# Four attention layers, a mixer block and an expert layer on one core: scores in pairs, table load, latent turns, rotation and the experts' opening reordered

## The chip, the cores and the metric

One Trainium2 chip, one of its cores. The metric is the device time of one execution in microseconds, median of several. The profile of one execution stands beside it. Engines: TensorE (PE; its weight loads are PEld), VectorE (DVE), ScalarE (ACT), GpSimd (POOL) and SyncE (SP), which only issues DMAs here.

## The reference

256 tokens of width 1024, fp32. Four layers, each `x = layernorm(alpha * x + branch(x))`: MLA, windowed attention (SWA), forget-gated attention (FoX), MLA again. All have 16 heads and a silu gate ahead of the closing product.

```
MLA:   h = x @ w_in            -> latents cq (384), ckv (256), k_rope (32), gate (1024)
       q = rmsnorm(cq) @ w_q_up ; k, v = rmsnorm(ckv) @ w_kv_up ; the last 32 columns of
       q (per head) and k_rope are rotated ; causal softmax attention ; (o * silu(gate)) @ w_out
```

Then a second block: `h = modulate(x)` (rmsnorm, times gain and 1 + scale, plus shift, where scale and shift come from a conditioning product), a projection to pool input, q, k, v and gates, block attention over 8 heads (MoBA; with 256 tokens it is plain causal attention), a pool mixer, the merged product and `x = x + gate1 * (merged @ w_out)`. Last the experts (PEER): `h2 = modulate(x)`, `q = h2 @ w_q` (16 halves of 128), scores of each half against 128 keys, the top 16 of each, the top 16 of their sums, and then gelu of products with 16384 expert rows, gated and multiplied by the second table, and a final rmsnorm.

## The kernel before

All weights come as one stream of chunks (128 x 4 x 512), issued by SyncE in halves, the *pieces*. A piece is split into a high and a low part for exact fp32 products out of three fp32r products: ScalarE copies it to `w_hi` (L1210), VectorE subtracts to `w_lo` (L1526), TensorE multiplies (L698 to L700). There are four places for split pieces (RING); a piece is split as soon as TensorE has dropped the piece four earlier. What each engine does between splits is written out by hand: each engine has its own program, and the order in it is the order of the work. `evacuate(unit)` splits ahead until the unit's last piece, copies the unit out of its PSUM banks, and splits one further piece; `evacuate_only` copies alone; `split_ahead(n)` splits up to piece n + 4. `pieces_behind(closing, n)` is the nth piece behind a closing unit.

A `Unit` is one stretch of TensorE's work with one or two PSUM banks of a pair; units alternate between two pairs, and `bank_free` makes TensorE wait until the unit that had the pair before is copied. A unit of kind token has tokens on the partitions, of kind feature the output columns; a `turn` unit is transposes of token-major data by 128 columns. Where the turned data feeds a product, its copy is a split too: ScalarE writes `xT_hi` (L1259), VectorE subtracts to `xT_lo` (L1560).

**MLA** (layers 0 and 3). After the opening projection the latents, five tiles of 128 columns, are turned as a unit of four tiles and one of one tile, the rotated key part beside the latter. TensorE waits for the unit of four, projects three query units (two pieces each) and four key/value units (one piece each), turns the queries (four units of four heads), and starts the scores once keys, values and the first turned queries are copied. VectorE's program interleaves the copies of key/value units 0 and 1 with the rotations of the queries of block 0 and 1 (six operations each, L1683 to L1688).

**Attention.** One loop over heads, on each engine. On TensorE, turn i of the loop: scores of head i + 1, turn of the probabilities of head i - 1 (L895), outputs of head i - 2 (L903 to L905). VectorE scales and masks the scores and takes the row maximum (L1638), ScalarE takes the exponential (L1279) and copies the turned probabilities (L1292), VectorE divides the outputs by the row sum (L1652). `scores` (L854) does one head, `pair_scores` (L839) two, its products alternating between the two halves of 64 rows. SWA and FoX have a third score bank and use pairs from head 4 on; MLA (96 rows) and MoBA use `scores`. In MoBA, ahead of the loop on TensorE: first scores, value projection, pool mixer product; in turns 2 to 8 of the loop one k-step each of the merged product (`project_half`). On ScalarE a split up to the value unit's last piece stands ahead of the loop.

**Closing and the experts' opening.** The closing product is one unit of both blocks for columns 0 to 511, then block 0 and block 1 for the right half (`project_closing`, four shared pieces). VectorE adds each to x (`gate1`, L1599 and L1600), ScalarE squares a whole row of x of one block and takes the root (`mean_square`, L1307), VectorE inverts it and does four operations per block (`modulate_block`: x times root times scale, twice; plus shift, twice; L1743, L1745), then TensorE turns each half of the block (L787). The layers open with `project_opening`: block 0's products run before block 1 is turned. The experts' queries don't: all four turned halves are waited for, then four feature units follow, and the scores against the keys (L1107).

## Time and profile before

| | us |
|---|---|
| time, median of 3 | 1605.41 (1602.81 to 1608.67) |
| profiled execution, own time | 1602.43 |
| its span | 1600.6 |
| TensorE busy | 1529.7 |
| VectorE busy | 1095.5 |
| ScalarE busy | 811.1 |
| mean granted TensorE clock | 0.995 of full |

The span runs from the first to the last instruction. Layers 0 to 3 end at about 578 us, the mixer block at 752, the experts' queries at 809, their scores at 817; the selection of experts runs beside the first table's products until about 960. A matmul's busy time overlaps with the next one's, so starts are to be compared, not ends. A row of the timeline merges like instructions (x count); in brackets is the idle time of the engine before it and what ended it.

### The profile page before, as it was taken

Reading aid. Unit: us, or ns where it says so; the run is one execution under the profiler, and the core shown is the slowest. Engines: PE = TensorE matmul, PEld = TensorE weight load, DVE = VectorE, ACT = ScalarE, POOL = GpSimd, SP = SyncE. Lnnn points to the kernel's source line nnn. Section 1 sums busy time; section 2 is a strip of 40 time slices with the busy share of each in tenths; the row PEclk is TensorE's granted clock in tenths of the full one; section 3 lists DMA queues with packets and bytes.
Section 4 is the critical chain, followed back from the end, with each engine's and each line's share of the span. In section 5 each row is a group of like instructions: output and inputs, shape, how many; then the busy total and the mean of one; then the engine's idle time right before and its main releaser. Section 6 shows DMA issues by size and latency. Waiting matters only on the chain.

```text
span 1600.6 us, 30066 instructions
## 1 busy us (share of the span) xinstructions
PE 1529.7 (96%) x10694; PEld 1331.6 (83%) x10694; DVE 1095.5 (68%) x2204; ACT 811.1 (51%) x1352; POOL 79.7 (5%) x110
## 2 busy tenths in 40 slices
PE   6989999999998989998999999999999999999997
PEld 5867877896787768776999999999998888888886
DVE  3566656656667485458569997777778888865555
ACT  3665465446547544454356666334444444444554
POOL 1000600100010100000000000000000000000000
PEclk9999999999999999999999999999999999999999
DMA  6553654656356556424535556444444445465552
GB/s 244 180 170 118 224 184 140 218 187 235 132 183 212 197 176 237 152 91 160 197 132 174 180 171 204 150 157 160 163 161 158 164 164 170 164 244 195 195 190 101
DMA packets 78501, 281.44 MB, mean 176 GB/s; under 512 B 9408, under 2 KB 11488, under 8 KB 77152
## 3 DMA queue, kind: packets, MB, share of 16 engines
q1 hardware_dynamic: 74176, 261.97, 48.4%
q0 software_dynamic: 4256, 18.56, 3.4%
q8 instruction: 41, 0.67, 0.2%
q14 instruction: 28, 0.23, 0.0%
HBM read 277.31 MB, written 2.14 MB: 175 GB/s over the span
## 4 chain that ended last, share of the span: by engine, by line
PE 76%; DVE 16%; ACT 3%; issue 3%; DMA 2%; POOL 0%; ACTq 0%; DVEq 0%; POOLq 0%
PE banks L698 21%; PE banks L700 21%; PE banks L699 21%; DVE w_lo L1526 5%; PE banks L1131 3%; PE banks L895 2%; PE banks L854 2%; PE banks L815 1%; PE banks L793 1%; PE banks L905 1%; DMA arena<-x_spill 1%; PE banks L904 1%; DVE arena L2010 1%; ACT w_hi L1210 1%; PE banks L903 1%
## 5 line engine op out<-in xcount | busy, mean ns | idle before, releaser
L1210 ACT ACTIVATE w_hi<-raw 128x1024 fp32r<-128x1024 f32 x456 | 474.0, 1042 | 549.0 <-PE banks L700 518.8
L1526 DVE TENSOR_TENSOR w_lo<-raw,w_hi 128x1024 fp32r<-128x1024 f32 x456 | 547.5, 1205 | 268.6 <-ACT w_hi L1210 265.3
L698 PE MATMUL banks<-w_hi,xT_hi 128*128 128x512 f32 (+2 forms) x1140 | 444.1, 390 | 15.5 <-DVE w_lo L1526 11.4
L700 PE MATMUL banks<-w_hi,xT_lo 128*128 128x512 f32 (+2 forms) x1140 | 437.1, 383 | 0.0
L699 PE MATMUL banks<-w_lo,xT_hi 128*128 128x512 f32 (+2 forms) x1140 | 436.7, 383 | 0.0
L698 PE MATMUL banks<-xT_hi,w_hi 128*128 128x256 f32 x1392 | 397.7, 286 | 4.6 <-DVE w_lo L1526 1.7
L699 PE MATMUL banks<-xT_lo,w_hi 128*128 128x256 f32 x1392 | 394.2, 283 | 0.0
L700 PE MATMUL banks<-xT_hi,w_lo 128*128 128x256 f32 x1392 | 394.1, 283 | 0.0
L698 PEld LDWEIGHTS banks<-xT_hi,w_hi 128*128 128x128 f32 x1392 | 267.4, 192 | 6.5 <-issue 4.1
L699 PEld LDWEIGHTS banks<-xT_lo,w_hi 128*128 128x128 f32 x1392 | 267.6, 192 | 0.2
L700 PEld LDWEIGHTS banks<-xT_hi,w_lo 128*128 128x128 f32 x1392 | 267.3, 192 | 0.0
L698 PEld LDWEIGHTS banks<-w_hi,xT_hi 128*128 128x128 f32 x1140 | 215.3, 189 | 61.7 <-DVE w_lo L1526 8.9
L700 PEld LDWEIGHTS banks<-w_hi,xT_lo 128*128 128x128 f32 x1140 | 215.2, 189 | 42.9
L699 PEld LDWEIGHTS banks<-w_lo,xT_hi 128*128 128x128 f32 x1140 | 215.6, 189 | 40.0 <-issue 0.2
L2081 DVE TENSOR_TENSOR arena<-arena,banks 128x512 f32 (+1 forms) x64 | 44.1, 689 | 76.6 <-PE banks L1131 73.8
L2073 DVE TENSOR_TENSOR scratch<-scratch 128x512 bf16<-128x512 bf16 x192 | 69.8, 419 | 0.0
L1259 ACT ACTIVATE arena<-banks 128x512 f32<-128x512 f32 (+3 forms) x74 | 41.0, 578 | 56.1 <-PE banks L700 38.8
L1279 ACT ACTIVATE scratch<-scratch,neg_max 128x128 f32<-128x128 f32 (+1 forms) x144 | 63.6, 444 | 2.2 <-DVE neg_max L1638 2.1
L1131 PEld LDWEIGHTS banks<-scratch 128*128 128x128 bf16 x1536 | 50.0, 98 | 9.7 <-issue 8.3
L1292 ACT ACTIVATE scratch<-banks 128x384 f32<-128x384 f32 x72 | 35.1, 488 | 44.8 <-PE banks L895 44.5
L1131 PE MATMUL banks<-scratch 128*128 128x64 bf16 x1536 | 57.7, 193 | 0.0
L895 PEld LDWEIGHTS banks<-kept,scratch 128*128 128x128 f32 x216 | 22.5, 140 | 39.8 <-issue 21.2
(195 smaller groups left out, 1284.6 us busy)
## 6 DMA issues: line engine op xcount, KB each, us to landing
raw<-stream SPq DMA_DIRECT2D x490, 512.0 KB, 3.6
arena<-ln_in POOLq DMA_DIRECT2D x4, 1024.0 KB, 5.8
arena<-x_spill POOLq DMA_DIRECT2D x3, 1024.0 KB, 10.7
arena<-mod_rows POOLq DMA_DIRECT2D x2, 1536.0 KB, 8.1
raw<-stream SPq DMA_DIRECT2D x6, 256.0 KB, 4.0
arena<-g_in POOLq DMA_DIRECT2D x3, 512.0 KB, 11.8
raw<-stream SPq DMA_DIRECT2D x8, 160.0 KB, 2.4
arena<-arena POOLq DMA_DIRECT2D x2, 512.0 KB, 4.3
```

The costliest lines, as they stand in the source:

```text
L698: pe.matmul(out, stationary[0], moving[0], start=first, stop=False, **k)
L699: pe.matmul(out, stationary[0], moving[1], start=False, stop=False, **k)
L700: return pe.matmul(out, stationary[1], moving[0], start=False, stop=last, **k)
L895: mm = pe.transpose(banks[:, 6 + g % 2, c * P:(c + 1) * P], probs[:, g % 2, c * P:(c + 1) * P], ident)
L1131: mm = pe.matmul(banks[:, 4 + s // GATE_STEPS, t * HALF:(t + 1) * HALF], hot2[:, t // 2, :, t % 2], hot1[:, part, t // 2, :, t % 2], start ...
L1210: act.activation(part(w_hi[:, s]), part(half_raw(s), True), ACT.Copy).then_inc(piece_hi, 1)
L1259: act.activation(dst, src, fn).then_inc(evac_act, 1)
L1279: ins = act.activation(probs[:, g % 2, lo:hi], s_sb[:, g % 2, lo:hi], ACT.Exp, scale=-1.0, bias=neg_max[:, g % 4, b:b + 1], accum_out=row_ ...
L1292: act.activation(probsT[:, g % 2], banks[:, 6 + g % 2, 0:384], ACT.Copy).then_inc(probsT_ready, 1)
L1526: dve.tensor_tensor(part(w_lo[:, s]), part(half_raw(s), True), part(w_hi[:, s].bitcast(F32)), ALU.subtract).then_inc(piece_lo, 1)
L2073: ins = dve.tensor_tensor(hot1[:, part], match1, picks[2 + part].broadcast_to(mine), ALU.mult)
L2081: dve.tensor_tensor(mine, mine, banks[:, 4 + s // GATE_STEPS, 0:GT * HALF].rearrange("p (t n) -> p n t", t=GT), ALU.mult).then_inc(g_taken ...
```

## The change

Six edits, all of them in the order of work, none in what is computed.

1. Latents: turned in units of two, two and one tiles; the first query unit gets a wait between its two pieces.
2. MLA, VectorE: each rotation stands ahead of the copy of key/value unit 0 or 1; the split behind the last key/value copy is left to a later place.
3. A dummy exponential (`exponential_table`) on ScalarE: in MLA between the second and third turned query unit, in MoBA ahead of the loop.
4. Scores: SWA and FoX do heads 2 and 3 as a pair in turn 0; MoBA does all heads in pairs, with two banks, and a pair waits for both masks of the pair before. MoBA's split ahead of ScalarE's loop moves behind the second exponential.
5. The experts' opening: the squares go by halves, the left ones once the left columns are there; x times scale is taken before the root, one half of it on GpSimd, and one fused operation per half remains behind the root; splits of pieces are placed anew; the first query unit becomes a token unit opened by blocks.
6. That unit's queries are turned (four tiles) after the second query unit; scores wait accordingly.

```diff
@@ -268,7 +268,7 @@
-peer = dict(h=cut(6144, B, D), qT=cut(8192, 2 * PEER_HEADS, S), keys=cut(12288, 2 * PEER_HEADS * NKEYS),
+peer = dict(h=cut(6144, B, D), q=cut(18432, B, COLS), qT=cut(8192, 2 * PEER_HEADS, S), keys=cut(12288, 2 * PEER_HEADS * NKEYS),
@@ -291,6 +291,7 @@
+squares = cut(8192, B, D)
@@ -314,8 +315,8 @@
-def feature_units(dst, tiles, how=COPY2):
-    return [Unit(plan, "feature", [dst[:, t:t + 2], dst[:, t + 2:t + 4]], how, pieces=4) for t in range(0, tiles, 4)]
+def feature_units(dst, tiles, how=COPY2, t0=0):
+    return [Unit(plan, "feature", [dst[:, t:t + 2], dst[:, t + 2:t + 4]], how, pieces=4) for t in range(t0, t0 + tiles, 4)]
@@ -351,9 +352,11 @@
-        L["cT"] = split_turn_units(5)
-        L["krT"] = [Unit(plan, "turn", [mla["krT"][0:ROPE, 0:1]], [("act", "copy")], tiles=1, width=ROPE, pair=L["cT"][1].pair,
-                         at=1, after=(L["cT"][1].before,))]
+        first = Unit(plan, "turn", [(0, 2)], [("both", "split")], tiles=2)
+        other = Unit(plan, "turn", [(2, 4)], [("both", "split")], col0=2, tiles=2, pair=first.pair, at=1, after=(first.before,))
+        L["cT"] = [first, other, Unit(plan, "turn", [(4, 5)], [("both", "split")], col0=4, tiles=1)]
+        L["krT"] = [Unit(plan, "turn", [mla["krT"][0:ROPE, 0:1]], [("act", "copy")], tiles=1, width=ROPE, pair=L["cT"][2].pair,
+                         at=1, after=(L["cT"][2].before,))]
@@ -421,7 +424,10 @@
-E["q"] = feature_units(peer["qT"], 2 * PEER_HEADS)
+E["q"] = token_units(peer["q"], COLS)
+E["q"] += feature_units(peer["qT"], 4, t0=4)
+E["qT"] = turn_units(peer["qT"], 4)
+E["q"] += E["qT"] + feature_units(peer["qT"], 8, t0=8)
@@ -459,6 +465,7 @@
+scale_ready, h_scaled = sem("scale_ready"), sem("h_scaled")
@@ -666,6 +673,9 @@
+    pool.wait_ge(scale_ready, 1)
+    wait_put(pool, M["out"][2:3])
+    pool.tensor_tensor(peer["h"][:, 1, COLS:D], x_tok[:, 1, COLS:D], moba["mod"][:, 4, COLS:D], ALU.mult).then_inc(h_scaled, 1)
@@ -830,10 +840,10 @@
-        if h == 4:
+        if third is not None and h == 4:
...
-            pe.wait_ge(max_ready, g - 1 if h else g)
+            pe.wait_ge(max_ready, g - 1 if third is not None and h > 2 else g)
@@ -882,7 +892,7 @@
-    def attention(heads, q, k, v, ada=(), late=(), beside=(), gated=None, third=None):
+    def attention(heads, q, k, v, ada=(), late=(), beside=(), gated=None, third=None, paired=False):
@@ -911,9 +921,9 @@
-            if third is not None and i >= 3:
-                if i % 2 and i + 1 < heads:
-                    pair_scores(i + 1, q, k, third)
+            if paired:
+                if i in (0, *range(3, heads - 1, 2)):
+                    pair_scores(max(i + 1, 2), q, k, third)
@@ -969,7 +979,8 @@
-            for u in L["q_up"]:
+            project(L["q_up"][0], between=lambda: wait_put(pe, L["cT"][1:2]))
+            for u in L["q_up"][1:]:
@@ -1010,7 +1021,7 @@
-                      third=third_bank(L))
+                      third=third_bank(L), paired=True)
@@ -1031,7 +1042,7 @@
-                      ada=(4, 6, 8, 10, 12, 14), late=L["late"], gated=(l, attn["o"]), third=third_bank(L))
+                      ada=(4, 6, 8, 10, 12, 14), late=L["late"], gated=(l, attn["o"]), third=third_bank(L), paired=True)
@@ -1064,7 +1075,7 @@
-    first_scores(queries, keys)
+    first_scores(queries, keys, paired=True)
@@ -1074,7 +1085,8 @@
-    attention(MOBA_HEADS, queries, keys, lambda h, b: moba["v"][:, b, HD * h:HD * (h + 1)], late=M["mixT"], beside=M["pool"])
+    attention(MOBA_HEADS, queries, keys, lambda h, b: moba["v"][:, b, HD * h:HD * (h + 1)], late=M["mixT"], beside=M["pool"],
+              paired=True)
@@ -1092,11 +1104,12 @@
-    for n, u in enumerate(E["hT"]):
-        pe.wait_ge(h_half, 4 + n + 1)
-        turn(u, peer["h"])
-    wait_put(pe, E["hT"])
-    for u in E["q"]:
+    open_layer(E["q"][0], E["hT"], h_half, 4, peer["h"])
+    project(E["q"][1])
+    wait_put(pe, E["q"][0:1])
+    for u in E["qT"]:
+        turn(u, peer["q"])
+    for u in E["q"][3:]:
@@ -1260,7 +1273,7 @@
-    def attention(heads, kind, last=None, mix=None, beside=()):
+    def attention(heads, kind, last=None, mix=None, beside=(), behind=None):
@@ -1279,6 +1292,8 @@
+            if i == 1 and behind is not None:
+                behind()
@@ -1308,9 +1323,24 @@
+    def square_half(b, half):
...
+        c = slice(half * COLS, (half + 1) * COLS)
+        link(act.activation(squares[:, b, c], x_tok[:, b, c], ACT.Square, accum_out=small[:, 48 + 2 * b + half:49 + 2 * b + half]))
+        if half == 0:
+            link(act.activation(small[:, 52 + b:53 + b], small[:, 48 + 2 * b:49 + 2 * b], ACT.Identity, bias=small[:, 5:6],
+                                scale=1.0 / D))
+        else:
+            act.activation(small[:, 40 + b:41 + b], small[:, 49 + 2 * b:50 + 2 * b], ACT.Sqrt, bias=small[:, 52 + b:53 + b],
+                           scale=1.0 / D).then_inc(dev_ready, 1)
...
...
+    def exponential_table():
...
+        act.activation(small[:, 45:46], small[:, 4:5], ACT.Exp)
@@ -1350,7 +1380,10 @@
-            for u in L["kv_up"] + L["qT"]:
+            for u in L["kv_up"] + L["qT"][:2]:
+                evacuate(u)
+            exponential_table()
+            for u in L["qT"][2:]:
@@ -1395,8 +1428,9 @@
-    split_ahead(M["v"][0].pieces_done - 1)
-    attention(MOBA_HEADS, "moba", last=M["v"][0], mix=M["mixT"][0], beside=M["pool"])
+    exponential_table()
+    attention(MOBA_HEADS, "moba", last=M["v"][0], mix=M["mixT"][0], beside=M["pool"],
+              behind=lambda: split_ahead(M["v"][0].pieces_done - 1))
@@ -1406,14 +1440,18 @@
+    wait_put(act, M["out"][0:1])
+    for b in range(B):
+        square_half(b, 0)
+    pieces_behind(M["out"], 1)
...
-    mean_square(0)
-    for n in range(1, RING):
+    square_half(0, 1)
+    for n in range(2, RING):
...
-    mean_square(1)
+    square_half(1, 1)
@@ -1831,15 +1869,16 @@
-                evacuate(L["kv_up"][b])
...
-            for u in L["kv_up"][B:]:
-                evacuate(u)
+                evacuate(L["kv_up"][b])
+            evacuate(L["kv_up"][2])
+            split_ahead(L["kv_up"][3].pieces_done - 1)
+            evacuate_only(L["kv_up"][3])
@@ -1929,25 +1968,47 @@
+    dve.wait_ge(g2_loaded, 32)
+    dve.wait_ge(mod_loaded, 32)
+    gain_scale(moba["mod"][:, 4])
+    dve.sem_inc(scale_ready, 1)
...
-    dve.wait_ge(g2_loaded, 32)
-    dve.wait_ge(mod_loaded, 32)
-    gain_scale(moba["mod"][:, 4])
+    wait_put(dve, out[0:1])
...
+    left, right = slice(0, COLS), slice(COLS, D)
...
+    def scaled(b, c):
+        note(dve.tensor_tensor(peer["h"][:, b, c], x_tok[:, b, c], moba["mod"][:, 4, c], ALU.mult))
...
+    def rooted(b):
...
+        settle()
+        inverse_root(small[:, 40 + b:41 + b], small[:, 42 + b:43 + b])
+        if b:
+            dve.wait_ge(h_scaled, 1)
+        for c in (left, right):
+            dve.scalar_tensor_tensor(out=peer["h"][:, b, c], in0=peer["h"][:, b, c], scalar=small[:, 42 + b:43 + b],
+                                     in1=moba["mod"][:, 3, c], op0=ALU.mult, op1=ALU.add).then_inc(h_half, 1)
...
+    for b in range(B):
+        scaled(b, left)
...
-    wait_put(dve, out[0:2])
-    modulate_block(peer["h"], moba["mod"][:, 4], moba["mod"][:, 3], 0)
+    wait_put(dve, out[1:2])
+    scaled(0, right)
+    rooted(0)
+    pieces_behind(out, 1)
...
-    modulate_block(peer["h"], moba["mod"][:, 4], moba["mod"][:, 3], 1)
-    pieces_behind(out, 1)
+    pieces_behind(out, 3)
+    rooted(1)
+    pieces_behind(out, RING)
...
-    pieces_behind(out, RING)
```

## Rows read from the trace of the kernel before

**Rows 1.** The page: busy time (share) xinstructions by engine; then two instruction groups.

```profile
PE 1529.7 (96%) x10694; PEld 1331.6 (83%) x10694; DVE 1095.5 (68%) x2204; ACT 811.1 (51%) x1352; POOL 79.7 (5%) x110
...
L1210 ACT ACTIVATE w_hi<-raw 128x1024 fp32r<-128x1024 f32 x456 | 474.0, 1042 | 549.0 <-PE banks L700 518.8
...
L1526 DVE TENSOR_TENSOR w_lo<-raw,w_hi 128x1024 fp32r<-128x1024 f32 x456 | 547.5, 1205 | 268.6 <-ACT w_hi L1210 265.3
```

**Rows 2.** Windows of 20 us: length, busy time of each engine, PEclk, DMA.

```profile
840.00:860.00 20.00, 20.00 (x169) 20.00 (x168) 19.83 (x64) 14.23 (x18) 0.00 (x0) 1.00 0.51 170
```

**Rows 3.** Timeline, first MLA layer, latents: start, us, instruction [idle <-releaser].

```profile
60.91 1.62 DVE L1560 TENSOR_TENSOR xT_lo<-banks,xT_hi 128x512 fp32r<-128x512 f32 x3 [0.93 <-ACT xT_hi L1259]
...
62.45 0.48 PE L698 MATMUL banks<-w_hi,xT_hi 128*128 128x512 f32 x1 [1.70 <-DVE xT_lo L1560]
```

**Rows 4.** Timeline, first MLA layer, keys, values and turned queries.

```profile
81.22 0.42 DVE L1683 TENSOR_TENSOR arena<-arena 128x256 f32<-128x256 f32 x1
...
83.48 0.69 DVE L1575 COPY arena<-banks 128x512 f32<-128x512 f32 x1
...
84.28 0.36 PE L698 MATMUL banks<-xT_hi,w_hi 128*128 128x256 f32 x1 [0.65 <-issue]
...
88.43 1.05 PE L793 MATMUL banks<-kept,arena 128*96 128x128 f32 x8 [1.05 <-DVE arena L1575]
...
91.84 1.55 PE L854 MATMUL banks<-arena 96*128 96x128 f32 x8 [0.63 <-ACT arena L1259]
```

**Rows 5.** Timeline, first MLA layer, start of attention.

```profile
95.79 1.28 ACT L1279 ACT_TABLE_LOAD   x1
...
98.12 0.55 PE L895 MATMUL banks<-kept,scratch 128*128 128x128 f32 x3 [0.85 <-ACT scratch L1279]
```

**Rows 6.** Timeline, scores of window attention, and of block attention.

```profile
219.20 0.92 PE L854 MATMUL banks<-arena 64*128 64x128 f32 x4
...
221.42 0.47 ACT L1292 ACTIVATE scratch<-banks 128x384 f32<-128x384 f32 x1
...
222.75 0.93 PE L839 MATMUL banks<-arena 64*128 64x128 f32 x8
...
670.71 0.93 PE L854 MATMUL banks<-arena 64*128 64x128 f32 x8
```

**Rows 7.** Timeline of block attention, then one window (PE busy, PEclk, DMA).

```profile
687.36 0.89 PE L854 MATMUL banks<-arena 64*128 64x128 f32 x4 [1.12 <-issue]
...
699.03 0.92 PE L854 MATMUL banks<-arena 64*128 64x128 f32 x4
...
689.00:692.50 3.50, 3.50 (x12) 0.51 0.45 150
```

**Rows 8.** Timeline of the experts' opening, then one window.

```profile
748.11 1.06 ACT L1307 ACTIVATE arena<-arena 128x1024 f32<-128x1024 f32 x1 [4.75 <-DVE arena L1600]
...
752.42 0.69 DVE L1599 TENSOR_TENSOR scratch<-banks,arena 128x512 f32<-128x512 f32 x1
...
755.58 1.41 DVE L1743 SCALAR_TENSOR_TENSOR arena<-arena,small 128x512 f32<-128x512 f32 x2
...
757.65 1.97 PE L787 MATMUL banks<-kept,arena 128*128 128x128 f32 x8 [4.43 <-DVE arena L1745]
...
761.15 0.55 PE L698 MATMUL banks<-xT_hi,w_hi 128*128 128x256 f32 x1 [1.53 <-DVE xT_lo L1560]
...
760.50:764.00 3.50, 2.85 (x13) 0.50 0.61 208
```

**Rows 9.** Timeline: GpSimd's 512-column product; experts' query copies; first score product.

```profile
388.87 1.27 POOL L602 TENSOR_TENSOR arena<-arena 128x512 f32<-128x512 f32 x1 [36.41 <-DVE arena L1652]
...
797.27 0.69 DVE L1575 COPY arena<-banks 128x512 f32<-128x512 f32 x1 [0.56 <-PE banks L700]
...
808.79 0.69 DVE L1575 COPY arena<-banks 128x512 f32<-128x512 f32 x1 [0.56 <-PE banks L700]
...
809.64 0.57 PE L1107 MATMUL banks<-arena 128*128 128x128 f32 x3 [0.89 <-DVE arena L1575]
```

## The prediction

> **What bounds the kernel now.** I read the page first: TensorE is busy 1529.7 of 1600.6 us, so all that a reordering can win lies in the 71 us in which it is not, plus products that can be run side by side [rows 1]. Then the stretches of 20 us: from 820 us on TensorE is full, and VectorE sits at 19.8 of 20 us in the selection of experts (840 to 860) [rows 2]. Last the timeline, gap by gap, with what released TensorE. The reader is to see in each row the idle time in brackets: it is what an edit can remove at that place, and no more. Since every stage up to 820 us hands its end directly to the next one on TensorE, a gap closed there moves all that follows; the selection starts from the expert scores, so it moves too and takes nothing back.
>
> **Latents by two tiles** (two MLA layers). Eight transposes take 1.05 us [rows 4], so four take 0.5. Before, the first copy waits for all eight; now it waits for four. TensorE sat 1.70 us before the first query product, until VectorE had subtracted the second pair of tiles, begun at 60.91 [rows 3]. With ScalarE still copying the last gate columns, the chain starts about 0.45 us sooner. The wait put between the two query pieces buys nothing more: the first query unit lies in the bank pair of the second latent unit, and its own wait for free banks covers that unit already. 0.45 us per layer (0 to 1.0).
>
> **Rotation ahead of copies.** A rotation is six operations of 0.42 us, 2.2 us with their links [rows 4]. Now both stand ahead of the copies of keys and values: VectorE at about 77.8 rotates to 80.1, copies unit 0 (0.69) to 80.8, splits a piece (1.2 us [rows 1]) to 82.0, rotates to 84.3, copies unit 1 to 85.0. The bank of unit 1 is what the last unit waits for: it started at 84.28 after 0.65 idle [rows 4] and now starts at about 85.1, ending at 88.0 instead of 87.3. What is queued behind this wait is only that unit and the turns. But the copy of unit 2 is then over (86.9), the rotation too, and the turn of queries starts at 88.05 instead of 88.43. The second turn waits for ScalarE's key copy of the last unit until 89.4 instead of 90.16. The split that stood between the last value copy and the first query copy on VectorE is deferred, so the first scores, at 91.84 before, wait only for ScalarE's copy of the first queries, at about 91.1. Gain 0.75 per layer (bounds: loss of 0.8, if the late last unit is paid in full, to gain of 1.7, the idle of 1.05 and 0.63 together). The deferred split frees the landing place of the second piece-pair of conditioning weights, needed only at head 5, some 8 us later: no cost, about 1 us if that cover were gone.
>
> **Exponential's table ahead** (both MLA layers). The load takes 1.28 us at 95.79 and ScalarE's first exponential follows it at once; TensorE is idle 0.85 before it turns the first probabilities [rows 5]. The load now falls where ScalarE waits for turned queries (91.6 to 93.1). After it TensorE's own order is dense: 0.85 per layer (0 to 1.28). Together the MLA layers give 2 x (0.45 + 0.75 + 0.85) = 4.1 us. A rule speaks here: the Trainium skill (ScalarE: Activation LUTs, "What ACT_TABLE_LOAD costs") gives 1283 ns and about 1380 ns of drain for a switch. The trace agrees on the load and shows no drain: the exponential began by 97.1, as its result left TensorE free at 98.12. By the rule the load removed would be 2.66 us, but the idle time behind it, 0.85, still caps the sum. In the block attention the moved load was under the value projection anyway: nothing.
>
> **Paired scores.** One head's scores are 0.92 us of TensorE, two heads issued as a pair 0.93 [rows 6]: 0.9 us per pair if TensorE is the bound there. In the window and forget layers only heads 2 and 3 are newly paired. There TensorE's next need is ScalarE's copy of head 0's turned probabilities, 221.42 to 221.89 [rows 6], and ScalarE works without a break from its table load on; so 0 (0 to 0.9 each). In the block attention heads 0 and 1 already took 0.93 together, one behind the other in different halves of the array [rows 6]: 0. For heads 2 and 3 the wait that ends last is the one for the mixed pool tiles, which frees TensorE at 687.36 [rows 7]. It stays, but head 3's 0.9 us now lie ahead of it, in place of idle time: 0.9. Heads 4 to 7 are in the stretch where scores, turn, outputs and half projection follow one another without a gap (687.36 and 699.03 are such heads) [rows 7]: 2 x 0.85. The new wait (both masks of the pair before) has behind it the turn, the outputs and the half projection of its turn of the loop; the mask of head 3 needs only the exponential of head 1, which now is done before the value projection ends. Sum 2.6 (0.9 to 3.5). TensorE's clock was granted at 0.51, the 1.2 GHz level, from 689 to 692.5 [rows 7]; I leave that as it is, since the idle ahead of it stays about 1.4 us. If it went, 3.5 us at half the clock would give back 1.7 more.
>
> **The experts' opening.** Before: the second residual unit is ready at 752.42; two pairs of gating operations, a square of 1.06 us, root, two scalings and two shifts end in the third turn at 757.65, after 4.43 us idle; the products begin at 761.15, after 1.53 idle and at a clock of 0.50 until 764 [rows 8]. After, step by step. Block 0: ScalarE now takes a piece (1.04 us) before the right half's square, so that the root comes at about 750.1 and the half-ready signals at 751.1 and 751.9: in time for 752. VectorE then splits a piece (1.2) that it did not before, and starts the second residual at 753.1, 0.7 late; it ends at 754.5, the two subtractions for block 0 at 755.2 and 755.9. TensorE can now start block 0's products at 755.35: idle 2.2. Two more splits stand ahead of block 1's scaling (to 758.4), reciprocal and two fused operations (0.7 each, from 1.41 for two [rows 8]) give signals at 759.45 and 760.1. TensorE has three pieces' worth of block 0 to do (4.3 us plus 0.5 waiting for the second piece), so it arrives at about 760.0 and waits for nothing. Then the last piece's split (to 761.35) holds it 0.4, and the subtractions for block 1 end at 762.8. A unit is 808.79 - 797.27 = 11.52 us [rows 9], so block 1's half is 5.76 and the first unit ends at 768.5. Before, it ended one unit and the slow part later: three more units led to 808.79, so it ended at 774.2. That is 5.7 gained, less eight more transposes (1.05, clear of waits because the banks are the first unit's, copied long before), plus the 0.89 before the first score product, which now needs the unit before the last: 5.5 us. The added right-half product on GpSimd is like the one of 1.27 us [rows 9]: 754.6 to 755.9, wanted at 758.4; behind it on that queue stands only the spill of x, which is wanted after the scores, 50 us later. Were that cover gone, 1.3. The gain scaling (1.2) moves to where VectorE waits for pieces: 0. Bounds: 2.0, if block 1's splits and signals come 3 us late, to 7.0, if the 2.2 idle shrinks by VectorE's early split being free.
> A rule speaks against the GpSimd part: the Trainium skill (GPSIMD Engine Reference, "1. Specifications") says that GpSimd shares its SBUF interfaces with VectorE, with contention where VectorE reads two SBUF inputs. The subtractions that run then read one input from PSUM, and no row shows the collision; by the rule at its worst the 1.3 us would be added to VectorE's order and the whole sum be 10.9 instead of 12.2.
>
> **Sum.** 4.1 + 2.6 + 5.5 = 12.2 us. The profiled execution took 1602.4 us (span 1600.6 and 1.8 around it), so it would be 1590.2; the median of three was 1605.4, 3.0 above the profiled one. Against the median: 1593.2 us.
>
> **Rivals.**
> A. The low clock stays at the experts' opening. For it: idle of 4.43 brought it [rows 8]. Against: idle of 1.70 did not [rows 3], and 2.2 lies nearer to that. Price: the low level held from the third turn (1.97 us instead of 1.05 for eight transposes) until 764, some 7 us at half the clock [rows 8], so 3.5 us. Time 1596.7.
> B. The new order bites in the MLA layers (late last unit in full, -0.8, no gain before the scores) and the opening is bound by VectorE (2.0): 2 x (0.45 - 0.8 + 0.85) + 2.6 + 2.0 = 5.6. Time 1599.8. For it: VectorE gets three splits ahead of block 1's signals.
> C. The change does not do what it says where overlap was there before: the pairs give nothing (as for heads 0 and 1), MLA half, opening 2.0: 4.0, no more than the measurement can tell. Time 1601.4.
> D. Slower: TensorE stays at the low level through the experts' queries, because block opening breaks its activity up. Four units of 11.5 us at half the clock would add 46 us; it decides from 24.4 us at the low level on, where it eats the 12.2 us. Time with 35 us of it, 17.5 lost: 1610.7. Against: before, the clock came back 3 us after the products had begun, and they ran on without a break [rows 8].
>
> **Numbers.** Forecast 0.57, A 0.18, B 0.12, C 0.10, D 0.03. The forecast's own range, from the bounds, is 1590 to 1597. Holding the time 8 in 10, with a noise of the median of some 2.5 us: 1587.5 to 1600.0. About 0.3%, 4.8 us, is what a measurement can tell from no change; faster is the forecast, A and B but for a little: 0.86; same: 0.11; slower: D, 0.03.
>
> **What would show it.** The gap before the query products in MLA about 1.2 instead of 1.7; the first MLA scores 0.75 us plus that 0.45 earlier than 91.84; table loads ahead of the turned queries and no gap of 0.85; four pairs of 0.93 in block attention; third turn of the experts' opening without 4.4 us idle, no 0.50 clock there, first unit done about 16.5 us after the last residual product. The prediction is wrong if the idle time merely moves to the next wait, above all if TensorE waits for split pieces in the opening.

## The result

The changed kernel takes 1589.01 us (median of 4 runs, 1586.35 to 1591.61), the kernel before 1604.74 (median of 4). The ratio is 0.9897, with a 95% interval of 0.9883 to 0.9912: 16.5 us less by the ratio, 15.7 by the two medians. The forecast was 1593.2, the range 1587.5 to 1600; the narrower range that the prediction calls its own was 1590 to 1597, and the time lies 1 us below it. A later set of four runs gave a median of 1589.56 and a ratio of 0.991 (0.9893 to 0.9926); the median of all eight is 1589.56 too. The first profiled execution took 1586.35 us, its span 1584.0, against 1602.43 and 1600.6 before; it is the fastest of the eight, so what is read from its profile is what this one execution did.

The busy line of the changed kernel's page, to be laid beside [rows 1]: TensorE is busy 8 us less (two products of a pair run side by side, and less work falls into a stretch at the low clock); the rest of the 16.6 is idle time. The window that answers to [rows 2] is as full as it was.

```profile
PE 1521.7 (96%) x10653; PEld 1325.5 (84%) x10654; DVE 1094.8 (69%) x2204; ACT 812.7 (51%) x1362; POOL 80.9 (5%) x111
```

```profile
823.00:843.00 20.00, 20.00 (x169) 20.00 (x168) 19.83 (x66) 13.87 (x17) 0.00 (x0) 1.00 0.51 164
```

Timeline of the changed kernel, first MLA layer (start, duration, instruction, and in brackets the idle time with what released it), to be laid beside [rows 3 to 5]. The reader is to see the 1.70 us become 0.97, the 0.65 before the last kv unit become 1.00, the turn of queries without its 1.05, the table load ahead at 91.00, and the first probabilities without their 0.85.

```profile
62.16 0.47 PE L708 MATMUL banks<-w_hi,xT_hi 128*128 128x512 f32 x1 [0.97 <-DVE xT_lo L1598]
...
84.58 0.36 PE L708 MATMUL banks<-xT_hi,w_hi 128*128 128x256 f32 x1 [1.00 <-issue]
...
87.53 1.03 PE L803 MATMUL banks<-kept,arena 128*96 128x128 f32 x8
...
90.55 1.58 PE L864 MATMUL banks<-arena 96*128 96x128 f32 x8 [0.48 <-ACT arena L1272]
...
91.00 1.28 ACT L1343 ACT_TABLE_LOAD   x1
...
95.84 0.49 PE L905 MATMUL banks<-kept,scratch 128*128 128x128 f32 x3
```

Window and forget attention ([rows 6]): the pair of eight products is there, and two new idles stand behind it.

```profile
216.97 0.93 PE L849 MATMUL banks<-arena 64*128 64x128 f32 x8
...
218.87 0.55 PE L905 MATMUL banks<-kept,scratch 128*128 128x128 f32 x3 [0.49 <-ACT scratch L1292]
...
219.72 0.43 PE L913 MATMUL banks<-arena,scratch 128*128 128x64 f32 x2 [0.30 <-ACT scratch L1307]
```

Block attention ([rows 6, 7]): four pairs, one idle of 1.39, and the clock at 1.00 where it had been 0.51.

```profile
678.61 0.93 PE L849 MATMUL banks<-arena 64*128 64x128 f32 x8
...
681.40 0.52 PE L905 MATMUL banks<-kept,scratch 128*128 128x128 f32 x3 [1.39 <-issue]
...
683.91 0.93 PE L849 MATMUL banks<-arena 64*128 64x128 f32 x8
...
689.70 0.93 PE L849 MATMUL banks<-arena 64*128 64x128 f32 x8
...
682.00:689.00 7.00, 7.00 (x47) 5.70 (x47) 3.89 (x23) 4.86 (x16) 0.00 (x0) 1.00 0.24 77
```

The experts' opening ([rows 8, 9]). VectorE's early split (741.48) holds the last residual copy until 742.62, 0.5 late (0.7 foreseen; 752.42 before, less the 10.34 gained up to here); the products start after 2.66 us idle and run on without another wait, at full clock; the first score product has no 0.89 ahead of it.

```profile
741.48 1.22 DVE L1564 TENSOR_TENSOR w_lo<-raw,w_hi 128x1024 fp32r<-128x1024 f32 x1
...
742.62 0.68 DVE L1637 TENSOR_TENSOR scratch<-banks,arena 128x512 f32<-128x512 f32 x1
...
744.18 1.26 POOL L678 TENSOR_TENSOR arena<-arena 128x512 f32<-128x512 f32 x1 [19.88 <-DVE arena L1638]
...
744.24 1.29 DVE L1598 TENSOR_TENSOR xT_lo<-banks,xT_hi 128x512 fp32r<-128x512 f32 x2 [0.21 <-DVE arena L1638]
...
745.19 0.47 PE L708 MATMUL banks<-w_hi,xT_hi 128*128 128x512 f32 x1 [2.66 <-DVE xT_lo L1598]
...
750.51 0.50 PE L708 MATMUL banks<-w_hi,xT_hi 128*128 128x512 f32 x1
...
745.00:755.00 10.00, 9.81 (x46) 7.87 (x47) 7.05 (x10) 3.28 (x6) 1.00 (x2) 1.00 0.75 277
...
793.07 7.20 PE L1120 MATMUL banks<-arena 128*128 128x128 f32 x63
```

The two traces as a ledger. A stage's gain is how much the difference of starts, before minus after, grows across it; the two last columns put back one part of the change at a time (below), from the same places of its profile and from its median, against 1589.56. A median is the weaker measure here: the 95% interval of the opening's ratio below, 0.9912 to 0.9956, is 7 us wide.

| stage | predicted | two profiles | put back, profile | put back, median |
|---|---|---|---|---|
| start, to 59 us | 0 | -0.15 | | |
| MLA, first | 2.05 | 2.43 | 2.37 | both: 5.9 |
| window attention | 0 | -0.08 | 0.0 | both: -0.4 |
| forget attention | 0 | 1.03 | 0.15 | |
| MLA, second | 2.05 | 2.59 | 2.55 | |
| block attention | 2.6 | 4.5 | 6.1 | 4.6 |
| experts' opening | 5.5 | 6.2 | 6.4 | 4.1 |
| after it | 0 | 0.1 | | |
| sum | 12.2 | 16.6 | | |

The sum is the span's difference, 1600.6 less 1584.0. To be explained are 0.9 us that were not expected of MLA, 1.0 that forget attention should not have had, 1.9 in block attention and 0.7 at the opening.

### The profile page after: what moved, and what is told of

It is laid out like the page before. It is cut to its first block, busy times and chain, and to the rows that moved or that the text cites. A ratio compares the mean times of both kernels' runs of the same rounds, so it can differ in the third digit from the quotient of the medians.

```text
span 1584.0 us, 30009 instructions
## 1 busy us (share of the span) xinstructions
PE 1521.7 (96%) x10653; PEld 1325.5 (84%) x10654; DVE 1094.8 (69%) x2204; ACT 812.7 (51%) x1362; POOL 80.9 (5%) x111
## 4 chain that ended last, share of the span: by engine, by line
PE 80%; DVE 14%; ACT 2%; issue 2%; DMA 0%; POOL 0%; ACTq 0%; DVEq 0%; POOLq 0%
PE banks L708 23%; PE banks L710 22%; PE banks L709 22%; DVE w_lo L1564 5%; PE banks L1144 3%; PE banks L905 2%; PE banks L864 1%; PE banks L825 1%; PE banks L803 1%; PE banks L915 1%; PE banks L914 1%; PE banks L849 1%; DVE arena L2071 1%; PE banks L913 1%; ACT w_hi L1223 1%
## 5 line engine op out<-in xcount | busy, mean ns | idle before, releaser
L708 PE MATMUL banks<-w_hi,xT_hi 128*128 128x512 f32 (+2 forms) x1156 | 450.1, 389 | 16.8 <-DVE w_lo L1564 10.8
L710 PE MATMUL banks<-w_hi,xT_lo 128*128 128x512 f32 (+2 forms) x1156 | 443.2, 383 | 0.0
L709 PE MATMUL banks<-w_lo,xT_hi 128*128 128x512 f32 (+2 forms) x1156 | 442.5, 383 | 0.0
L708 PE MATMUL banks<-xT_hi,w_hi 128*128 128x256 f32 x1360 | 388.1, 285 | 3.9 <-issue 2.0
L709 PE MATMUL banks<-xT_lo,w_hi 128*128 128x256 f32 x1360 | 384.6, 283 | 0.0
L710 PE MATMUL banks<-xT_hi,w_lo 128*128 128x256 f32 x1360 | 384.5, 283 | 0.0
L708 PEld LDWEIGHTS banks<-xT_hi,w_hi 128*128 128x128 f32 x1360 | 260.6, 192 | 5.9 <-issue 5.2
L709 PEld LDWEIGHTS banks<-xT_lo,w_hi 128*128 128x128 f32 x1360 | 260.8, 192 | 0.2
L710 PEld LDWEIGHTS banks<-xT_hi,w_lo 128*128 128x128 f32 x1360 | 260.6, 192 | 0.0
L1690 DVE TENSOR_TENSOR arena<-banks,row_sum 128x128 f32<-128x128 f32 x72 | 21.0, 292 | 48.9 <-PE banks L915 48.1
```

Source lines behind the costliest of these rows:

```text
L708: pe.matmul(out, stationary[0], moving[0], start=first, stop=False, **k)
L709: pe.matmul(out, stationary[0], moving[1], start=False, stop=False, **k)
L710: return pe.matmul(out, stationary[1], moving[0], start=False, stop=last, **k)
```

## The experiments

Each kernel is the changed one with the edit shown; the profiled execution of each is read by the same stages. "Late" is how much later than in the first profile of the changed kernel something starts. Where only one run is given, the stages of its profile count and not its time.

**The opening put back.** Both edits of the opening are undone: token queries by whole units, ScalarE's and VectorE's old order, eight transposes fewer.

```diff
-            open_layer(E["q"][0], E["hT"], h_half, 4, peer["h"])
+            for n, u in enumerate(E["hT"]):
+                pe.wait_ge(h_half, 4 + n + 1)
+                turn(u, peer["h"])
+            wait_put(pe, E["hT"])
...
-            rooted(0)
-            pieces_behind(out, 1)
+            modulate_block(peer["h"], moba["mod"][:, 4], moba["mod"][:, 3], 0)
```

> Both edits of the experts' opening are undone (the queries' unit again by whole tokens, the pieces' splits and the eight transposes back in their old order); the layers keep the new order. If the opening is worth what the two traces show between the end of the MoBA projection and the first score product of the experts, this runs 6.2 us over the changed kernel (5.5 by the prediction). The stretch at the low clock ahead of the experts' queries should be back if it hangs on VectorE's whole-token unit: then 6 to 7 us, with a wait of over 4 us on the products' operand. If the low clock stays away without the edit, 4 to 5 us and the rest of the gain belongs to the clock. Nothing of it should be given back later: the last product should end by the same difference.

Measured: 1593.64 us (median of 5, ratio to before 0.9934, 0.9912 to 0.9956), 4.1 over the changed kernel. Its profile is 1.05 late at the end of the MoBA projection and 7.44 at the first score product: 6.4. The timeline and a window of that stretch:

```profile
748.35 1.82 PE L791 MATMUL banks<-kept,arena 128*128 128x128 f32 x8 [4.43 <-DVE arena L1772]
...
751.70 0.55 PE L702 MATMUL banks<-xT_hi,w_hi 128*128 128x256 f32 x1 [1.53 <-DVE xT_lo L1587]
...
749.00:754.50 5.50, 3.97 (x19) 3.60 (x18) 5.32 (x6) 1.19 (x2) 0.00 (x0) 0.50 0.36 119
```

The idle of 4.43, the slow turn and the low clock are back exactly as in [rows 8]. Nothing is given back later (7.5 at 944 us).

**Whole-token queries in the new order.** Here only the block opening is undone; pieces and roots keep their new order.

```diff
-            open_layer(E["q"][0], E["hT"], h_half, 4, peer["h"])
+            for n, u in enumerate(E["hT"]):
+                pe.wait_ge(h_half, 4 + n + 1)
+                turn(u, peer["h"])
+            wait_put(pe, E["hT"])
+            project(E["q"][0])
```

> The experts' queries' unit keeps the new order of the work ahead of it but opens by whole tokens, not by blocks. If the blocks give most of the gain (the prediction: products start 5.8 us earlier), products start some 3 to 5 us later than in the changed kernel, and the first score product of the experts 3 to 4 us later. If the low clock ahead of the experts' queries hangs on the length of that wait, it comes back and adds 1 to 2 us. Rival: the shorter chain of the root gives most: 1 to 2 us and no low clock.

Measured: 1595.47 us in one run. The products start 7.1 us later than in the changed kernel (753.19 less the 0.93 by which this profile was late before the stage, against 745.19), the first score product 8.2, and the wait at 953.00 (943.81 in the changed kernel) 8.3. That is twice what was expected, 3 to 5 and 3 to 4.

```profile
749.69 1.97 PE L797 MATMUL banks<-kept,arena 128*128 128x128 f32 x8 [6.18 <-DVE arena L1996]
...
753.19 0.76 PE L708 MATMUL banks<-w_hi,xT_hi 128*128 128x512 f32 x1 [1.53 <-ACT xT_hi L1276]
...
749.00:758.00 9.00, 6.78 (x19) 5.37 (x20) 3.82 (x5) 1.20 (x2) 0.00 (x0) 0.50 0.62 218
```

That is worse than the old opening (6.4): the two splits ahead of block 1 make a whole-token turn later, 6.18 idle instead of 4.43, and pay only where block 0's products cover them. The low level also lasts longer, about 10 us for 6.8. The blocks are the gain; what is left of the two edits without them is a loss of 1.8 (8.2 against 6.4), and the rival falls. The squares by halves and the early scaling were not put back by themselves.

**GpSimd's product back on VectorE.**

```diff
-            pool.wait_ge(scale_ready, 1)
-            wait_put(pool, M["out"][2:3])
-            pool.tensor_tensor(peer["h"][:, 1, COLS:D], ...).then_inc(h_scaled, 1)
...
+            scaled(1, right)
```

> Only the product of the right half of the second token tile goes back from GpSimd to VectorE, 0.7 us of VectorE's time. If VectorE's order sets the start of the experts' queries, they start 0.7 us later and so does the first score product of the experts. Rival: VectorE waits at that place for something else (the reciprocal's root or the last product), and it costs 0 to 0.2. A shared way into the memory for the two engines, had it been paid in the changed kernel (its product took 1.26 us beside two of VectorE's subtractions), would make VectorE's part shorter here: under 0.5 us.

Measured: 1591.04 us in one run, and from 3.28 to 3.91 late across the opening, 0.63. But not where it was expected: the queries start with the same idle, and the product of 0.68 pushes the split behind it, for which TensorE waits 0.52 in front of the second piece.

```profile
747.52 1.29 DVE L1595 TENSOR_TENSOR xT_lo<-banks,xT_hi 128x512 fp32r<-128x512 f32 x2 [0.21 <-DVE arena L1635]
...
748.72 0.68 DVE L1980 TENSOR_TENSOR arena<-arena 128x512 f32<-128x512 f32 x1
...
748.47 0.47 PE L705 MATMUL banks<-w_hi,xT_hi 128*128 128x512 f32 x1 [2.65 <-DVE xT_lo L1595]
...
750.59 0.50 PE L705 MATMUL banks<-w_hi,xT_hi 128*128 128x512 f32 x1 [0.52 <-DVE w_lo L1561]
```

VectorE's two subtractions take 1.29 us here, without GpSimd's product, and 1.29 beside it in the changed kernel (744.24, above), so running beside each other cost nothing. The Trainium skill (GPSIMD Engine Reference, "1. Specifications") tells of contention where VectorE reads two SBUF inputs; each of these subtractions reads one of its inputs from PSUM (`banks`), so that case is not tested here.

**Block attention put back,** then its two parts. First all of it:

```diff
-            first_scores(queries, keys, paired=True)
+            first_scores(queries, keys)
...
-            exponential_table()
-            attention(MOBA_HEADS, ..., behind=lambda: split_ahead(M["v"][0].pieces_done - 1))
+            split_ahead(M["v"][0].pieces_done - 1)
+            attention(MOBA_HEADS, ...)
```

> MoBA alone is undone: each head's scores singly again, the exponential's table and the piece split in their old order; MLA, SWA, FoX and the opening of the experts keep the new order. Theory: the 4.5 us that this layer gained in the traces are 2.6 us of edits and some 1.5 to 1.9 us of a low-clock stretch that the edits remove, so it runs 4.5 us over the changed kernel and the low clock at about 683 us is back. Rival: the low clock was a matter of where the stretch fell in the execution, and it stays away: 2.6 to 3 us over. Second rival: ScalarE's copies are the need in all of it, as in SWA: 0 to 1 us.

Then the pairs alone (the first part of that edit and `paired=True` of the attention loop), and ScalarE's order alone (the second part):

> In MoBA only the pairing of the scores is undone; ScalarE's work keeps the new order (the table ahead, the piece split behind). The prediction gives the pairs all of the MoBA gain: 0.9 for heads 2 and 3, 0.85 each for two of the later pairs, 2.6 us, and the low clock at about 683 us with them. The layer's edits undone together cost 6.1 us in the traces, low clock included. Theory: the pairs are 2.6 us plus the clock, so 4 to 6 us from the first scores to the end of the projection, with the low clock back. Rival: the order on ScalarE carries a part: under 2 us and no low clock.

> In MoBA only ScalarE's order is undone (the split of the weights' piece ahead of the heads again, the table not ahead); the pairs stay. Theory: the order of ScalarE lies under TensorE's turns, 0 to 0.5 us from the first scores to the end of the projection, and no low clock. Rival: the 1.9 us that MoBA gained over the 2.6 of the prediction are ScalarE's: 1 to 2 us later, with idle ahead of the first turn of probabilities and the low clock at about 683 us back.

Measured: all of it 1594.13 us (median of 5, ratio 0.9939, 0.9914 to 0.9965), 4.6 over, and 6.1 in its profile; the pairs alone 6.0 (one run, 1595.06); ScalarE's order 0.2 (one run, 1589.48). All of the layer's gain is the pairs'. The low clock is back with single scores, and earlier than before; with the pairs kept and ScalarE in its old order (third block) it is not:

```profile
682.13 1.52 PE L864 MATMUL banks<-arena 64*128 64x128 f32 x4 [1.12 <-issue]
...
683.00:688.50 5.50, 5.50 (x18) 3.89 (x17) 1.77 (x11) 2.23 (x9) 0.00 (x0) 0.50 0.29 98
```

```profile
683.07 1.50 PE L864 MATMUL banks<-arena 64*128 64x128 f32 x4 [1.40 <-issue]
...
683.00:690.00 7.00, 6.93 (x22) 5.27 (x23) 2.71 (x11) 2.51 (x10) 0.00 (x0) 0.51 0.25 77
```

```profile
683.07 0.52 PE L905 MATMUL banks<-kept,scratch 128*128 128x128 f32 x3 [1.12 <-issue]
```

Three profiles now have single scores, with the low level for about 3.4, 6.8 and 6.8 us (summed over windows of 2 us), and the layer costs 4.5, 6.1 and 6.0 us more than with pairs. So nearly 0.5 us is lost per us at the low level ((6.1 - 4.5) / (6.8 - 3.4)), and what is left without it is about 2.9 us, where the prediction had 2.6. Rows at the full clock give the same 2.9: two single heads take 2 x 3.39 us (in the kernel before, 695.64 below to 699.03 in [rows 7]), two paired ones 5.79 (683.91 to 689.70 above), so a pair is worth 0.99, not 0.85, twice, and heads 2 and 3 give the 0.9.

```profile
695.64 0.92 PE L854 MATMUL banks<-arena 64*128 64x128 f32 x4
```

In none of the eleven profiles with pairs was the clock low between 676 and 720 us. What keeps it up isn't the idle time ahead. The cleanest comparison is ScalarE's old order with pairs and without: both have 1.12 us of idle and the same busy time of TensorE in the 6 us ahead of the next product (4.53 and 4.56), and only without pairs is the clock low behind it. In the changed kernel it is 1.39 idle and 4.61 busy, with the pairs alone undone 1.40 and 4.67. The windows of the changed kernel, of all put back, and of ScalarE's order put back:

```profile
675.40:681.40 6.00, 4.61 (x26) 3.31 (x25) 3.64 (x7) 3.29 (x7) 0.00 (x0) 1.00 0.57 197
```

```profile
676.10:682.10 6.00, 4.56 (x22) 3.19 (x21) 3.49 (x7) 5.99 (x16) 0.00 (x0) 1.00 0.43 152
```

```profile
677.07:683.07 6.00, 4.53 (x26) 3.19 (x25) 3.48 (x7) 5.99 (x16) 0.00 (x0) 1.00 0.45 156
```

One thing in them does go with the edit: the number of products, 26 with pairs, 22 or 23 without, since a pair puts eight score products where one head has four. No run shows whether that is the cause.

**MLA put back,** all three edits, then two of them singly.

```diff
-                    for u in L["kv_up"] + L["qT"][:2]:
-                        evacuate(u)
-                    exponential_table()
-                    for u in L["qT"][2:]:
+                    for u in L["kv_up"] + L["qT"]:
                         evacuate(u)
...
                     for b in range(B):
+                        evacuate(L["kv_up"][b])
...
-                        evacuate(L["kv_up"][b])
-                    evacuate(L["kv_up"][2])
-                    split_ahead(L["kv_up"][3].pieces_done - 1)
-                    evacuate_only(L["kv_up"][3])
+                    for u in L["kv_up"][B:]:
+                        evacuate(u)
```

> The MLA edits are undone (latents by one tile, rotation behind the copies, the exponential's table behind the queries' units), in both MLA layers. The prediction had 4.1 us for the two; the traces show 2.45 and 2.55 from the layer's start to its end, so this runs 4.9 us over the changed kernel. Rival: part of what the first layer shows is the clock at the start of the execution, which differs between the two profiles: then the sum is 4 us or less, and the idle of 1.70 us ahead of the queries' opening is not all back.

> Only the exponential's table in the two MLA layers is undone (loaded again behind all four queries' units). By the prediction's step the first turn of probabilities waits again, idle of 0.85 us ahead of it in each layer, so it starts 0.85 us later against the layer's first scores; from the layer's start to its end 0.85 each, 1.7 in both. Rival: with the rotation ahead the queries' units end earlier on ScalarE too, so part of the load is hidden: 0 to 0.5 each. A drain of 1.4 us in front of the load, had ScalarE one, would put it at 1.28 plus 1.38 behind the last copy: over 1.5 us of idle instead of 0.85.

> Only the order of VectorE's work behind the rotation in MLA is undone (the rotation of the kv tiles and queries again behind the copies). The prediction had 0.75 us per layer of this edit: the wait ahead of the last kv unit goes from 1.00 back to 0.65 us, 0.45 ahead of the queries' turns comes back (1.05 us of idle), and the first scores start later. The traces say 1.29 less 0.29, about 1.0 us at the first scores. So 0.75 to 1.0 per layer later at the first scores. Rival: the gain is carried by the table, and with it ahead the first probabilities start no later: 0 at the layer's end.

Measured: all three 1595.44 us (median of 6, ratio 0.994, 0.9921 to 0.9959), 5.9 over; its profile has 2.37 and 2.55 in the two layers, and 1.2 of a low clock at the experts' opening that is not the edit's. The table alone (1591.16 us, one run) costs 1.00 and 1.16; the rotation alone (1589.74, one run) 0.97 at the first probabilities of the first layer (in the second, a low clock at 506 to 511 us lies over it). The rest, 0.45, is the latents by two tiles, which were not put back by themselves: from the latents' turn to the query opening the profile of all three put back goes from 0.61 to 1.06 late, and those of the two single edits stay as late as they were. First the table's rows, then the rotation's:

```profile
95.04 1.28 ACT L1292 ACT_TABLE_LOAD   x1
...
97.37 0.55 PE L905 MATMUL banks<-kept,scratch 128*128 128x128 f32 x3 [0.76 <-ACT scratch L1292]
```

```profile
83.48 0.36 PE L708 MATMUL banks<-xT_hi,w_hi 128*128 128x256 f32 x1 [0.65 <-issue]
...
87.63 1.05 PE L803 MATMUL banks<-kept,arena 128*96 128x128 f32 x8 [1.04 <-DVE arena L1613]
```

The load starts when the activation before it ends, and takes 1.28; TensorE waits 0.76, but 1.00 is lost: with the table ahead the probabilities' turn starts 0.76 behind the start of the scores before it (95.08 to 95.84), here 1.67 (95.70 to 97.37). The products' own 0.92 overlaps with what follows when nothing waits, and the idle in brackets does not count that 0.15. A drain beside the load, of which the Trainium skill speaks (ScalarE: Activation LUTs, "What ACT_TABLE_LOAD costs"), is in no row: the activation ahead of the load ends at 95.02, the load starts at 95.04, and the exponential behind it at 96.34.

**The pair of heads 2 and 3** in window and forget attention put back.

```diff
-                    if paired:
+                    if third is not None and i in (0, 2):
+                        scores(i // 2 + 2, q, k)
+                    elif paired:
```

> Only the pair of heads 2 and 3 in SWA and FoX is undone; all else is the changed kernel. Theory: ScalarE's copy of head 0's probabilities is the need of the product behind, so the pair gives nothing (0 in both layers), and the 1.03 us that FoX gained in the traces are the raw pieces of the weights that landed late in the profile before: the same time as the changed kernel within 0.3 us. Rival: the pair gives FoX its 1.0 us and more would come in SWA without its waits: 1.0 us over the changed kernel, with idle of 0.28 and 0.30 us ahead of the two probability turns gone.

Measured: 1589.11 us (median of 4, ratio 0.9899, 0.9869 to 0.9929), no difference; across window attention 0.0, across forget attention 0.15, with the two idles gone. The singly issued score at 219.34 fills the wait that the pair leaves:

```profile
219.34 0.92 PE L864 MATMUL banks<-arena 64*128 64x128 f32 x4
...
220.76 0.43 PE L913 MATMUL banks<-arena,scratch 128*128 128x64 f32 x2
```

**The changed kernel again, and three more moves.** The repeat shows what belongs to an execution.

> The changed kernel again, beside the next one on the same chip: 15 to 16.5 us under the kernel before. It serves as the mark for the next kernel, and its profile shows which of the differences between the two first profiles belong to the execution: the low clock at 24 to 28 us, and the 1.03 us in FoX. If FoX's 1.03 is of the edits, its stage takes as long as in the first profile of the changed kernel (98.70 us from 283.25 to 381.95); if it is the landing of the weights' pieces, it takes anything from 98.7 to 99.8.

Forget attention took 98.70 us in the first profile of the changed kernel and 99.47 in the repeat; others with the same code of this layer took between 98.7 and 99.7 where the clock stayed up, the kernel before 99.78. What differs is ScalarE's wait for weights that the stream has not landed. The same piece in the kernel before, in the repeat, and in the first profile, where it had landed and TensorE's banks were the wait:

```profile
372.72 1.06 ACT L1210 ACTIVATE w_hi<-raw 128x1024 fp32r<-128x1024 f32 x1 [2.60 <-DMA raw<-stream]
```

```profile
370.03 1.06 ACT L1223 ACTIVATE w_hi<-raw 128x1024 fp32r<-128x1024 f32 x1 [2.24 <-DMA raw<-stream]
```

```profile
369.58 1.06 ACT L1223 ACTIVATE w_hi<-raw 128x1024 fp32r<-128x1024 f32 x1 [1.66 <-PE banks L710]
```

So some 0.9 of the 1.1 us by which the stage differs is landing (2.60 less 1.66), not the change. The repeat also had a low clock at the experts' opening that the first profile had not; it lost 1.3 us there (0.66 late at the turn ahead of it, 1.98 at the first score product):

```profile
747.00:750.00 3.00, 3.00 (x9) 2.19 (x8) 2.96 (x6) 0.00 (x0) 0.00 (x0) 0.52 0.99 350
```

Another stretch cost nothing. At the opening of the block attention layer TensorE waits 4.5 us in every profile, and in all fourteen the clock is low behind it, for some 3.4 us in eight and 6.8 in six. The first profile of the changed kernel, then the repeat:

```profile
574.00:577.00 3.00, 3.00 (x10) 2.13 (x9) 2.96 (x6) 1.20 (x2) 0.00 (x0) 0.50 0.00 0
```

```profile
574.00:580.00 6.00, 5.58 (x13) 3.43 (x14) 5.96 (x10) 2.81 (x6) 0.00 (x0) 0.51 0.00 0
```

The repeat is 0.70 late at the start of this opening (574.42 against 573.72) and 1.69 at the turn behind the low stretch (584.71 against 583.02), but again 0.69 at the first scores (665.60 against 664.91): the first profile waits 0.78 for a split piece behind the turn and the repeat does not, which takes up most of the 1.0.

Then three further moves (the second kv copy ahead of the second rotation, a split ahead of block 0's root, the exponential's table ahead of the last split in window and forget attention):

```diff
+                        if b:
+                            evacuate_only(L["kv_up"][1])
                         rotate(...)
...
             scaled(0, right)
-            rooted(0)
             pieces_behind(out, 1)
+            rooted(0)
...
                     for u in L["gate"] + L["kv"] + L["q"][:1]:
                         evacuate(u)
+                    exponential_table()
```

> Three further moves in the same manner on top of the changed kernel: in MLA the copy of the second kv unit ahead of the second rotation (the wait of 1.00 us ahead of the last kv unit goes: 1.0 us per layer, 2.0 in both, if nothing is late behind it); in the experts' opening the split of the second block moved ahead of the root, with no subtraction behind the last product (0.65 us); in SWA and FoX the exponential's table ahead of the last piece split (0 to 1.2 us each, the nearest wait ahead of their first turn of probabilities is 0.6 to 1.2). Sum 2.7 to 5.0 us under the changed kernel, 3.5 taken. Rival: the rotation is late for the queries when a copy is put ahead of it, and MLA gives back what the kv unit gains: 0.7 to 1.5 us under. Second rival: TensorE's turns behind are bound by the same evacuations, and it gives nothing.

Measured on one chip, four runs each, with no overlap between the two sets: 1584.94 us (1581.20 to 1586.40) against 1589.56 (1589.09 to 1591.55); ratios to before 0.988 (0.9864 to 0.9897) and 0.991. It is the fastest version, 4.6 us under the changed kernel. By its profile 1.3 in each MLA layer, 0.8 in window attention, 0.05 in forget attention, 0.9 at the opening, 4.4 in all (2.7 to 5.0 expected):

```profile
85.99 1.05 PE L803 MATMUL banks<-kept,arena 128*96 128x128 f32 x8
...
87.72 1.05 PE L803 MATMUL banks<-kept,arena 128*96 128x128 f32 x8 [0.68 <-DVE arena L1615]
...
216.11 0.87 PE L905 MATMUL banks<-kept,scratch 128*128 128x128 f32 x6
...
374.73 0.40 ACT L1292 ACTIVATE scratch<-scratch,neg_max 128x128 f32<-128x128 f32 x1 [0.41 <-DVE neg_max L1678]
...
740.52 0.47 PE L708 MATMUL banks<-w_hi,xT_hi 128*128 128x512 f32 x1 [1.74 <-DVE xT_lo L1600]
```

The 1.00 before the last kv unit is gone (the 0.68 behind the first turn is new), the pair's two turns in window attention now follow one another (x6, 0.87), and the experts' queries wait 1.74 instead of 2.66. Forget attention gains nothing from the same move: its idles vanish too, but ScalarE now waits 0.41 for VectorE's row maxima (374.73). The exponential there starts 2.57 us ahead of the changed kernel's (377.30), while the layer itself had started 2.52 ahead: nothing was won in between.

## Why the prediction was right, and where it was not

- Latents by two tiles: 0.45 said, 0.45 measured. The two traces alone would have said more (1.70 to 0.97). Put back, the idle is 1.23 but the start moves by 0.45 only, and profiles with the new code show 0.81 to 1.42 of idle there at the same distance from the turn ahead; the start is the thing to read.
- Rotation ahead of copies: the mechanism came as written (last unit later, 0.65 to 1.00 idle; turn of queries without its 1.05). Said 0.75, measured 0.97. The late unit costs 0.35 to 0.6, not 0.8, and the first scores gain 1.0 against the query opening (91.84 - 62.45 = 29.39 before, 90.55 - 62.16 = 28.39 after), not 0.74.
- Table ahead: said 0.85, measured 1.00 and 1.16. The idle in brackets was taken as the whole cost; the overlap of 0.15 that a wait breaks comes on top.
- Pairs in window and forget attention: 0 said, 0 measured; the idle that appears instead shows that ScalarE is the need. The 1.0 of forget attention is nearly all late landing in the profile before.
- Pairs in block attention: said 2.6, measured 2.9 at the full clock (0.99 for each of the later pairs, not 0.85). The step that failed is "I leave that as it is, since the idle ahead of it stays about 1.4 us". The idle did stay (1.39), and the clock did not fall: the 1.7 us named behind it came (1.6).
- The experts' opening: start of the products 755.35 said, 755.5 on the old time scale (745.19 and the 10.34 gained before); the 0.5 and 0.4 us of waits foreseen behind it did not come; end 6.2 earlier against 5.5. The sum, counted from the first unit's end, held the slow part of the old opening in it. With 6.8 us at the low level at 0.39 us each (the repeat: 1.32 us lost in some 3.4), about 2.6 of the 6.2 to 6.4 is clock and 3.7 the order; this is an estimate from one stretch. GpSimd's product counted 0 with a cover of 1.3: worth 0.63.
- The range: "1590 to 1597" is said to come from the bounds, but those of the steps as they stand add to 1.3 and 20.3 us, so to 1585 to 1604. The result lies outside the narrow range and inside the wide one.
- Rival A was half right: the low level came in 3 of the 11 profiles with the new opening, but costs 1.3 us, not 3.5, and so can't be seen in the median. B and C fall with MLA (4.9 where they had 1.0 and half of 4.1) and the opening; D since in every profile the clock was up again within 6 us of the products' start.

**How much is the clock.** By the forecast's own terms the two traces gained 4.9 to 5.0 in MLA (4.1 said), 2.9 by the pairs (2.6) and 6.2 at the opening (5.5, the slow part of the old opening included): 14.0 to 14.1 for 12.2. On top come the 1.6 of the low stretch in block attention, which the forecast put at nothing, and 1.0 in forget attention, nearly all landing: 16.6 to 16.7. Clock in both places is then some 1.6 + 2.6 = 4.2 us. The mean granted clock was 0.991 over 19 runs of the kernel before and 0.995 over 8 of the changed one, some 29 and 16 us at the low level (twice the missing share of the span). Over the 19 runs a us of it goes with 0.34 us of time, which would make 4.3 of the 15.9 us between their mean times. That this is the same size does not show that it is the same stretches: the profiled execution of the kernel before, at 0.995, had few of them, and where the others had theirs no profile shows.

What stays open: why single scores bring the low clock in block attention and pairs do not. It follows the edit (3 of 3 against 0 of 11); idle and busy time ahead of it do not differ, the number of products does, and nothing here tests it. The profiles put back add to more than the whole (17.6 against 16.6, mainly since the low stretch in block attention was longer in them), the medians to less (14.2 against 15.7, within their intervals).

## What to carry to other kernels

Read each gap in brackets as what one edit can win there, then ask whether the clock falls behind it. A stretch at the low level cost 0.4 to 0.5 us per us here where TensorE was the need, and nothing in the end where a later wait for split pieces took it up; the length of the gap ahead did not tell whether it would come. Pairing products pays only where TensorE is the need; where an idle appears in place of the saved time, the releaser's other work (a table load, a copy, a split) may be moved ahead of it. That gave 0.8 us in window attention and 0.05 in forget attention, where the next releaser was right behind; what share the pair has in the 0.8 was not tested. An order that put splits ahead of a late operand paid here only with work by blocks to cover it. Take a gain from two profiles only after a second profile of the same kernel: the landing of weights moved one stage by up to 1 us.

## What was not expected of the hardware

Whether the clock falls at a place changes between executions even where the code there is the same: besides the single scores, the opening of the experts and that of the block attention layer, it was low at 24 to 28 us in ten of the fourteen profiles, though not in the one before nor in the repeat, at 378 to 384 in two (forget attention took 100.3 and 101.6 us there) and at 640 to 646 in two (1.6 us). At the experts' opening a stretch of some 3.4 us at the low level lost 1.32 us; between the heads of block attention nearly 0.5 us per us; at that layer's opening 3.4 us more of it lost 1.0 us, all of which was back by the first scores; over whole runs 0.34 us per us.
